# Forget logits of a hybrid attention layer taken with the sink heads' values, and their cumulative sums spread by transfers

## The reference

```python
proj = x @ w_in
fq, fk, fv = ...                      # 8 heads x 64 each, forgetting attention
ff = proj[..., OFF_FF:OFF_SQ] + b_forget      # 8 columns: one forget logit per head and token
sk = rope(...)                        # 2 key heads x 64 of the sink (sliding-window) group
sv = ...                              # 2 value heads x 64 of the same group

c = cumsum(log_sigmoid(ff), axis=tokens)
s = q.k * scale + c[query] - c[key]   # causal, then softmax, then times fv
```

## Time and profile before

| | |
|---|---|
| time, median of 3 runs | 2770.1 us (2766.78 to 2772.87) |
| time of the profiled execution | 2776.75 us |
| its span | 2774.9 us |
| TensorE busy | 2598.7 us (94%) |
| VectorE busy | 2251.6 us (81%) |
| ScalarE busy | 912.4 us (33%) |
| GpSimd busy | 1309.0 us (47%) |
| first scores of pair 0 (end of the first stage) | 95.97 us after the start |

### The profile page before, as it was taken

One profiled execution on the slowest core, in us unless ns is written; L12 is line 12 of the kernel. 1 busy time (PEld: TensorE's weight loads), 2 busy tenths in 40 slices (PEclk: granted clock), 3 DMA queues, 4 the chain that ended last, 5 costly groups with the idle time before them and its releaser, 6 DMA issues.

```text
span 2774.9 us, 45831 instructions
## 1 busy us (share of the span) xinstructions
PE 2598.7 (94%) x17059; PEld 1687.8 (61%) x17251; DVE 2251.6 (81%) x4526; ACT 912.4 (33%) x1606; POOL 1309.0 (47%) x864
## 2 busy tenths in 40 slices
PE   8999979999988877899999999999999999999996
PEld 3677646689977765555565565565564564664653
DVE  4244556658789999788989988988998999999998
ACT  3333334521125556432222232232232322331324
POOL 2110010000034442266766766766666677676772
PEclk9999989999999999999999999999999999999998
DMA  4000212320103355999999999999999999999995
GB/s 165 24 16 17 84 61 98 131 99 14 38 22 130 133 209 220 326 382 361 359 353 382 355 355 351 365 373 354 347 375 356 365 373 372 345 380 367 348 342 208
DMA packets 277917, 690.68 MB, mean 249 GB/s; under 512 B 29896, under 2 KB 112328, under 8 KB 273488
## 3 DMA queue, kind: packets, MB, share of 16 engines
q0 software_dynamic: 110592, 402.70, 38.6%
q1 hardware_dynamic: 167120, 285.25, 29.0%
HBM read 626.99 MB, written 60.88 MB: 248 GB/s over the span
## 4 chain that ended last, share of the span: by engine, by line
PE 27%; DVE 19%; DMA 15%; issue 12%; POOL 3%; ACT 1%; SPq 1%; DVEq 0%; ACTq 0%; POOLq 0%
PE h_psum L1748 9%; DMA early<-u_blocks 6%; PE o_psum L2228 6%; PE r_t_psum L1211 5%; PE g_psum L2228 4%; DVE early L2069 3%; DMA early<-v_blocks,pick_index 3%; DVE rt_hot L1647 3%; POOL early L1755 2%; DMA early<-v_blocks 2%; PE h_psum L1261 2%; DVE wide L2073 2%; DMA early<-u_rows,pick_index 2%; DMA fetched<-u_rows,pick_index 1%; DVE early L1738 1%
## 5 line engine op out<-in xcount | busy, mean ns | idle before, releaser
L1748 PE MATMUL h_psum<-early 128*128 128x384 bf16 x5496 | 767.3, 300 | 6.6 <-DVE early L1738 3.4
L1748 PEld LDWEIGHTS h_psum<-early 128*128 128x128 bf16 x5496 | 537.7, 98 | 234.3 <-issue 10.1
L1755 POOL DMA_INDIRECT early<-u_rows,pick_index x320 | 456.9, 1428 | 227.8 <-DVE dots L2069 142.3
L1755 POOL DMA_INDIRECT early<-v_blocks,pick_index x320 | 459.5, 1436 | 199.3 <-DVE wide L2073 117.3
L2228 PE MATMUL o_psum<-v_split,w_split 128*128 128x512 bf16 x2293 | 543.0, 382 | 1.6 <-issue 0.2
L2073 DVE SCALAR_TENSOR_TENSOR wide<-early,dots,wide 128x1024 f32<-128x1024 f32 x320 | 405.5, 1279 | 23.5 <-DMA early<-v_blocks,pick_index 22.0
L2069 DVE CUSTOM_DVE_ANT_0 early<-early,wide 128x1024 f32<-128x1024 f32 x320 | 386.9, 1218 | 30.3 <-DMA early<-u_rows,pick_index 27.5
L2228 PEld LDWEIGHTS o_psum<-v_split,w_split 128*128 128x128 bf16 x2304 | 227.2, 99 | 277.2 <-issue 9.1
L2228 PE MATMUL g_psum<-v_split,w_split 128*128 128x512 bf16 x1399 | 348.8, 384 | 35.6 <-DVE w_split L2035 12.6
L2228 PEld LDWEIGHTS g_psum<-v_split,w_split 128*128 128x128 bf16 x1536 | 150.0, 98 | 198.0 <-issue 31.1
L1947 ACT ACTIVATE v_split<-early 128x512 bf16<-128x512 f32 x256 | 159.0, 622 | 320.9 <-PE o_psum L2228 217.5
(11 more groups left out here) (230 smaller groups left out, 3335.1 us busy)
## 6 DMA issues: line engine op xcount, KB each, us to landing
early<-v_blocks SPq DMA_DIRECT2D x256, 256.0 KB, 6.4
early<-u_blocks SPq DMA_DIRECT2D x115, 512.0 KB, 8.4
gates<-wide SPq DMA_DIRECT2D x20, 2048.0 KB, 6.4
gate<-gates SPq DMA_DIRECT2D x31, 1280.0 KB, 21.4
early<-w_query SPq DMA_DIRECT2D x8, 1024.0 KB, 5.9
rt_u_pre<-u_blocks SPq DMA_DIRECT2D x13, 512.0 KB, 4.0
early<-w_fox SPq DMA_DIRECT2D x4, 1536.0 KB, 6.4
early<-u_rows,pick_index POOLq DMA_INDIRECT x320, 8.3
```

Source lines behind the costliest of these rows:

```text
L1748: mm = pe.matmul(bank(half)[:, 0:width * P], u_split[:, k, part, c], xs[:, first:first + width, xpart, c, :], start=(c == 0 and part == 0 ...
L1755: pool.indirect_dma_start(row, None, source, bass.IndirectOffsetOnAxis(ap=pick_index[:, tile, at:at + 1], axis=0)).then_inc(arrived, 16)
```

## The change

Host side: `b_forget` is handed over repeated for the eight token tiles, `minus_row` is gone, and there is a DRAM scratch tensor `neg_c_rows` of 8 x 1024 fp32. In the first stage:

- The first loop of TensorE makes the keys alone. The forget weights stand beside the value weights in `w_vf` (136 columns), so that the values' matmuls bring 8 logits for each tile of tokens, with tokens on partitions; three tiles share a bank.
- The value and forget weights have a semaphore of their own, `w_vf_in`; `const_in` counts eight loads.
- Softplus runs on 128 partitions x 64 columns. Eight transposes then bring it to 8 partitions x 1024 in `s_psum[1]`, from where the scan reads it. Sums now have the sign of `neg_c`, and `c_col` is copied with scale -1.
- SP stores the scan's rows to `neg_c_rows` and loads each row back with a broadcast over 128 partitions; VectorE waits for two heads ahead of pair 0 (`bias_in[0]`) and for six ahead of pair 1.
- Odd chunks of pair 0's projection go to `t_psum[1]`, even ones to `p_psum`; a chunk of pair 0 waits for the copy of the chunk two before it.
- The rotation stands ahead of chunk 0; the projection's other five chunks are one run.

```diff
+VF = P + FOX_HEADS
+VF_TILES = 3
...
+        vf_psum = [bank[:, 0:VF_TILES * VF].rearrange("p (t n) -> p t n", n=VF)
+                   for bank in (t_psum[0], t_psum[1], s_psum[0][:, 0])]
...
+        def chunk_bank(pair, chunk):
+            return t_psum[1] if pair == 0 and chunk % 2 else p_psum
...
             def _(sp):
-                sp.dma_start(w_f_raw[:, :, :], w_forget).then_inc(w_first_in, 16)
...
-                sp.dma_start(w_kv_raw[:, 1], w_skv[:, 1]).then_inc(const_in, 16)
-                sp.dma_start(b_f[:, :], b_forget).then_inc(const_in, 16)
+                sp.dma_start(w_kv_raw[:, 1], w_skv[:, 1]).then_inc(w_vf_in, 16)
+                sp.dma_start(w_f_raw[:, :, :], w_forget).then_inc(w_vf_in, 16)
+                sp.dma_start(f_bias, b_forget.partition_broadcast(P)).then_inc(const_in, 16)
...
-                sp.dma_start(minus_row, consts["minus_row"]).then_inc(const_in, 16)
...
                 for n in range(3):
                     load_weights(n)
+                sp.wait_ge(first_ready, 2)
+                sp.dma_start(neg_c_rows, c_row).then_inc(c_stored, 16)
+                sp.wait_ge(c_stored, 16)
+                for h in range(FOX_HEADS):
+                    sp.dma_start(neg_c[:, h], neg_c_rows[h].partition_broadcast(P)).then_inc(bias_in[int(h >= 2)], 16)
...
             def _(pe):
-                        if c == 0 and past(n):
-                            pe.wait_ge(chunk_copied, n)
+                        if c == 0 and n > 1:
+                            pe.wait_ge(chunk_copied, n - (n < FOX_CHUNKS))
...
-                        f_mm = products(s_psum[0][0:FOX_HEADS, half], lambda a: w_f[:, a, c], x_half,
-                                        c == 0, c == KD - 1)
-                        k_mm = products(s_psum[1][:, half], lambda a: w_kv[:, a, 0, c], x_half,
-                                        c == 0, c == KD - 1)
+                        mm = products(s_psum[1][:, half], lambda a: w_k[:, a, c],
+                                      lambda b: xt[:, b, c, half * 512:half * 512 + 512], c == 0, c == KD - 1)
...
-                        mm = products(t_psum[t // 4][:, t % 4 * P:t % 4 * P + P],
-                                      lambda a: xt[:, a, c, t * P:(t + 1) * P], lambda b: w_kv[:, b, 1, c],
+                        mm = products(vf_psum[t // VF_TILES][:, t % VF_TILES],
+                                      lambda a: xt[:, a, c, t * P:(t + 1) * P], lambda b: w_vf[:, b, c],
                                       c == 0, c == KD - 1)
...
-                project_fox(0, 0, 0, KD)
-                pe.wait_ge(const_in, 16 * 10)
...
+                project_fox(0, 0, 0, KD)
+                pe.wait_ge(f_step, 7)
                 pe.wait_ge(first_ready, 1)
-                for h in range(FOX_HEADS):
...
-                        mm = pe.matmul(s_psum[h % 2][:, half], minus_row[:, h], c_row[:, half * 512:half * 512 + 512],
-                                       start=True, stop=True)
-                    mm.then_inc(bcast_done, 1)
-                    project_fox(0, 0, 2 * KD + h * KD // 2, 2 * KD + (h + 1) * KD // 2)
+                for t in range(TILES):
+                    mm = pe.transpose(s_psum[1][0:FOX_HEADS, t // 4, t % 4 * P:t % 4 * P + P], f_rows[:, t], ident)
+                mm.then_inc(first_made, 1)
+                pe.wait_ge(first_copied, 7)
+                project_fox(0, 0, KD, FOX_CHUNKS * KD)
+                pe.wait_ge(first_ready, 2)
...
             def _(dve):
+                dve.wait_ge(first_copied, 1)
+                dve.tensor_tensor(sk_t[:, :], raw[:, :], cos[:, :], ALU.mult).then_inc(rope_step, 1)
+                dve.wait_ge(first_copied, 4)
+                dve.tensor_tensor(f_flat, f_flat, f_bias, ALU.add).then_inc(f_step, 1)
...
+                dve.wait_ge(first_made, 3)
+                dve.tensor_tensor(rope_tmp[:, :], s_flat[1], sin[:, :], ALU.mult).then_inc(rope_step, 1)
+                dve.wait_ge(rope_step, 2)
+                dve.tensor_tensor(sk_t[:, :], sk_t[:, :], rope_tmp[:, :], ALU.add).then_inc(first_ready, 1)
+                dve.wait_ge(f_step, 6)
+                dve.tensor_tensor(f_flat, f_tmp, f_flat, ALU.subtract).then_inc(f_step, 1)
+                dve.wait_ge(first_made, 4)
...
+                dve.tensor_tensor_scan(c_row, s_flat[1][0:FOX_HEADS], zeros, 0.0, ALU.add, ALU.add).then_inc(first_ready, 1)
...
+                    if u == 0 and pair < 2:
+                        dve.wait_ge(bias_in[pair], (32, 96)[pair])
                     dve.wait_ge(scores_done, n + 1)
...
             def _(act):
-                for h in range(FOX_HEADS):
-                    act.wait_ge(bcast_done, h + 1)
...
-                    act.activation(neg_c[:, h], s_flat[h % 2], ACT.Copy).then_inc(bcast_copied, 1)
...
+                for chunk in range(FOX_CHUNKS):
+                    copy_chunk(0, 0, chunk)
+                act.wait_ge(first_made, 5)
```

More of the change, by code:

```diff
@@ L271, in project_fox @@
                             pe.wait_ge(pair_lo, pair + 1)
-                        if c == 0 and past(n):
-                            pe.wait_ge(chunk_copied, n)
-                        half = chunk % 2
+                        if c == 0 and n > 1:
+                            pe.wait_ge(chunk_copied, n - (n < FOX_CHUNKS))
+                        bank, half = chunk_bank(pair, chunk), chunk % 2
                         if chunk < 4:
-                            mm = products(p_psum[:, :], lambda a: w_pair[:, kp, a, chunk // 2, c],
+                            mm = products(bank[:, :], lambda a: w_pair[:, kp, a, chunk // 2, c],
                                           lambda b: xt[:, b, c, half * 512:half * 512 + 512], c == 0, c == KD - 1)
@@ L507, in rope @@
                     dve.tensor_tensor(rope_tmp[:, 0:512], p_psum[:, :], sin[:, part], ALU.mult).then_inc(chunk_copied, 1)
[L508 to L509 removed]
+                    dve.tensor_tensor(local.q_t[pair][:, part], raw[:, part], cos[:, part], ALU.mult).then_inc(rope_step, 1)
+                    dve.wait_ge(rope_step, n + 3)
                     dve.wait_ge(chunk_copied, FOX_CHUNKS * PAIRS + SWA_CHUNKS * pair + 3 + half)
@@ L637, in _ @@
-                act.wait_ge(fa_step, 1)
-                act.activation(f_tmp[2], f_tmp[2], ACT.Ln, bias=1.0).then_inc(fa_step, 1)
-                act.wait_ge(first_made, 2)
-                act.activation(raw[:, :], s_flat[1], ACT.Copy).then_inc(raw_copied, 1)
-                act.wait_ge(first_made, 3)
-                for k in range(2):
-                    act.activation(sv_rows[:, 4 * k:4 * k + 4].rearrange("p t c -> p (t c)"), t_psum[k][:, :],
-                                   ACT.Copy).then_inc(raw_copied, 1)
@@ L645, in _ @@
[L645 to L654 removed]
+                        act.wait_ge(w_first_in, 16)
@@ new lines, in _ @@
+                        act.activation(w_k[:, 0], w_kv_raw[:, 0], ACT.Copy).then_inc(w_hi, 1)
+                act.wait_ge(w_vf_in, 32)
+                act.activation(w_vf[:, 0, :, 0:P], w_kv_raw[:, 1], ACT.Copy).then_inc(w_hi, 1)
+                act.activation(w_vf[:, 0, :, P:VF], w_f_raw[:, :, :], ACT.Copy).then_inc(w_hi, 1)
+                act.wait_ge(first_made, 1)
+                act.activation(raw[:, :], s_flat[1], ACT.Copy).then_inc(first_copied, 1)
+                act.wait_ge(first_made, 2)
@@ new lines, in _ @@
+                for k, bank in enumerate(vf_psum):
+                    tiles = slice(VF_TILES * k, min(VF_TILES * (k + 1), TILES))
+                    act.activation(f_rows[:, tiles], bank[:, 0:tiles.stop - tiles.start, P:VF], ACT.Copy
+                                   ).then_inc(first_copied, 1)
+                for k, bank in enumerate(vf_psum):
+                    tiles = slice(VF_TILES * k, min(VF_TILES * (k + 1), TILES))
+                    act.activation(sv_rows[:, tiles], bank[:, 0:tiles.stop - tiles.start, 0:P], ACT.Copy
+                                   ).then_inc(first_copied, 1)
```

126 lines of the change are left out of this document (44 added, 82 removed).

## The result

The changed kernel takes 2732.3 us (median; 2725.4 to 2737.2) against 2768.4 for the kernel before on the same occasion; the ratio is 0.9866, 95% interval 0.9844 to 0.9888.

What follows compares the result with a forecast made beforehand. TensorE's own work list was taken to bound the first stage; 0.45 + 12.05 - 0.7 + 16.4 - 1.0 + 0.2 = 27.4 us, taken as 27.3, gives 2770.1 - 27.3 = 2742.8 us. Range 2737 to 2753 us, 77 in 100.

Steps and rivals of the forecast that it cites:

- Key loop: TensorE's first loop without forget products: ends at 22.2 us instead of 34.7, bounds 22.0 to 23.6; 12.05 in the sum.
- Values with 136 columns: Value matmuls carrying the forget logits: 11.6 us instead of 10.9, a cost of 0.7 us, ending at 33.8.
- Rotation and chunk 0: Behind the values: rotation some 1.9 us, chunk 0 5.0 to 5.1 us, no wait for POOL's first split, margin 1.6.
- Spread by matmul: TensorE's per-head spreads among pair 0's chunks go: 2.05 us a head, 16.4 us for eight, the largest term.
- Second bank: Own bank for pair 0's odd chunks: prevents a new wait of about 0.7 us at each of four boundaries.
- Spread by DMA: SP's store and broadcasts, first two heads in at about 64 us, needed at 69.3: cost taken as zero.
- biases late: Rival, 7 in 100: broadcasts ahead of pair 0 as slow as under load, first bias at 73.5 us, time 2747 us.
- Port held by POOL: Rival, 7 in 100: late softplus subtraction held until POOL's second split ends at 49.4; 8.9 us given back, 2752 us.
- Clock: Rival, 3 in 100: pauses in the first loop keep TensorE at 1.2 GHz until the first scores; slower, 2799 us.
- Sum: All first-stage terms: 27.4 us by addition, 27.2 by the clock of pair 0's first bias, 27.3 taken.
- 3 us either way for a median of three runs (2766.8 to 2772.9): Allowance in the forecast range for uncertainty of the starting time, the median 2770.1 us.
- nothing in this stage is a share of the whole: Ground for taking the first-stage saving worked out in the profiled execution, unscaled, from the median of the runs, 2770.1 us.

Runs made afterwards that it cites:

- e1: The changed kernel as it is, run again against the kernel before: ratio 0.9875 (0.9836 to 0.9913).
- e9: The changed kernel as it is, another repeat against the kernel before: ratio 0.9885 (0.9853 to 0.9918).
- e4: The kernel before with its matmul spreads and their copies cut to 128 of 1024 columns, leaving wrong biases: ratio 0.9948 (0.9921 to 0.9974) to the kernel before.
- e7: The changed kernel with all chunks of pair 0 in one bank: ratio 0.9910 (0.9882 to 0.9938) to the kernel before.
- e8: The changed kernel with the eight broadcasts issued from head 7 down to head 0: ratio 0.9907 (0.9884 to 0.9931) to the kernel before.
- e5: The kernel before, making forget products for the first slice of x alone: ratio 0.9949 (0.9926 to 0.9973) to the kernel before.
- e6: The changed kernel with ScalarE waiting for all constants before casting the values' weights: ratio 0.9926 (0.9900 to 0.9951) to the kernel before.
- the first comparison: The changed kernel's first measurement against the kernel before: 2732.3 us against 2768.4, ratio 0.9866 (0.9844 to 0.9888).
- e10: The changed kernel as it is, another repeat against the kernel before: ratio 0.9886 (0.9851 to 0.9920).
- e3: The kernel before plus only the changed kernel's DRAM scratch and one awaited store to it: ratio 0.9985 (0.9960 to 1.0010) to the kernel before.
- e2: The changed kernel with 128 additional 512-column matmuls on TensorE ahead of chunk 1: ratio 1.0003 (0.9977 to 1.0030) to the kernel before.
- e11: The changed kernel with 128 additional 512-column matmuls ahead of chunk 1, a repeat: ratio 0.9984 (0.9962 to 1.0007) to the kernel before.
- e12: The changed kernel with 512 additional 512-column matmuls ahead of chunk 1: ratio 1.0304 (1.0266 to 1.0343) to the kernel before.

## Why the prediction was right in the stage and wrong in the number

- **Which stage, and what bounds it:** right. TensorE's list stayed without a gap, and first bias and end of list moved together.
- **Key loop:** forecast to end at 22.2, the values began at 21.9. 36 of its matmuls in e1 went in 7.95 us (14.19 to 22.14), 0.66 us for three, so the additional 0.1 us of the earlier trace rows did belong to the alternation with the 8-row weights. TensorE started at 8.86, 0.5 earlier than the 9.35 assumed.
- **Values with 136 columns:** 11.35 us (21.88 to 33.23), forecast 11.6. **Rotation and chunk 0:** 2.0 and 5.0 us, no wait for POOL in this trace. The margin of 1.6 us was too thin to count on: it was 1.0 here, and in e1 and e9, where the weights landed later, TensorE waited 0.42 us. **Transposes:** 0.9 us to the next chunk, forecast 1.0. **Chunks 1 to 5:** 26.35 (41.06 to 67.41), forecast 26.0.
- **Spread by matmul, 16.4:** 16.1 by chunks 1 to 5 of the two traces, and e4 measures 1.5 of the 2.05 a head by itself. **Second bank:** 0.86 a boundary in e7, forecast 0.7.
- **Spread by DMA at nothing:** right. The store was followed by the first broadcast at 55.5 (forecast 57.5). The rival "biases late" had some 6 us of room in the order chosen: in e8 all eight were in at 71.35, six heads of 512 KB at 394 GB/s are 8.0 us, and the first broadcast was issued 0.6 later than in the changed kernel, which puts the first two at 62.8 there, an estimate, against 68.8.
- **Port held by POOL:** the wait of TensorE didn't come, since the chain ended 5.5 us clear of POOL's second subtraction. But the working left out the first one: the chain's first operation was held behind it in all four traces of the changed kernel, by 0.3 to 1.6 us, and only the chain's margin of about 2 us hid that. e5 shows the full price where the chain slips.
- **Clock:** the fear of a slow stage was wrong, since all from 14.1 us on went at full pace. The recorded 1.00 doesn't fit the start of the first loop, though: 11 matmuls of 512 columns fill 4.64 us there, 0.42 each, as at the lower level, while the earlier trace rows has this slow pace only until 12.58. It cost nothing, for x was awaited. Pauses of 2 and 4 us in e5 and e6 lowered the clock for a few microseconds, not for a stage.

```profile
8.86:13.50 4.64, 4.64 (x11) 1.64 (x12) 1.91 (x2) 1.84 (x3) 0.00 (x0) 1.00 1.03 418
```

- **Sum:** first bias forecast at 69.5, measured 68.8: 27.95 us saved there for 27.3. "Should reach the end nearly whole": 26.6 arrive at the end of routing.

The step that failed is the last one, from the stage to the time, with two terms in it. The first is the starting time and its room, "3 us either way for a median of three runs (2766.8 to 2772.9)", the spread of those three. Single executions of this kernel have a standard deviation of 7.4 us, and up to the end of routing traces of the same code agree within 1.4 us, so nearly all of it arises behind the routing. The three came out 4.6 high, and starting from 2765.5 the same saving gives 2738. The range should have had some 6 us either way for that alone: 5 for a median of three and 3.7 for a result of four executions, added as squares. The 5.5 us given as what a measurement can tell from no change is likewise less than one deviation of a single execution. The second term is "nothing in this stage is a share of the whole", which takes the expert phase as equal in both kernels: the saving over 22 and 71 executions is 32.2 us and not 27.3. The 10.5 us between 2742.8 and 2732.3 are then 4.6 of the start, 4.9 of the saving, and 1.0 by which the result's four executions lie below the mean of 22. That the start was high is chance, and it alone would have left the result inside the range; the additional saving is what no part of the working had.

What is left open is the cause of these 4.9 us, whose standard error is 1.5. That is over three standard errors, and by the means of their own occasions the differences are 37.0 (the first comparison), 32.0 (e1) and 32.2 (e9 and e10), so chance is an unlikely cause. Put as the expert phase alone (mean time, less 1.8 us outside the span, less the end of routing in the trace), the kernel before has 1634.8 us (standard error 0.9) and the changed kernel 1628.9 (1.2). Between them lie the scratch alone (e3) with 1631.9 (2.4), the delayed kernels with 1632.4 (e2 and e11, 1.7) and 1633.3 (e12, 4.0), and the changed kernels with their stage made longer (e6, e7, e8) with 1633.3 (1.6). Those three average 20.9, 23.5 and 26.4 us below the 2765.5 of before, where their traces have 20.0, 22.6 and 23.2 at the end of routing. The two kernels that leave out values have 1628.4 (e4, 1.6) and 1624.4 (e5, 2.8), though they have the code of before behind the stage; so a shorter phase isn't the changed kernel's alone, unless their wrong values cause it there. Layout, instruction list and time of the start each showed no effect beyond some two standard errors, and no trace locates the 4.9 us.

## What to carry to other kernels

Before a saving of a per cent is forecast, find the part of the kernel whose length changes from one execution to the next: here the first stage repeats within 1 us, while the expert phase, with a DMA share of 0.97 from 1140 us to the end, spreads over 20, so the range belongs to the latter and the sum to the former. A small operand that rides with a large one (8 columns on 128) cost 0.4 us here (11.35 for 10.94), while as weights of its own it took a full pass of x, some 12 us. When work that covered a copy or a landing is taken away, list what it covered: a second bank was worth 3.5 us here and a semaphore of its own 5.7, of which 1.5 was a late landing.

## What the runs showed of the hardware

- Behind a 2 us wait of TensorE (e5) and a 4 us wait (e6) its granted clock was 0.54 over 7.5 us and 0.57 over 4 us, costing 3 and 1.6 us on top of the wait. In e5 TensorE had been busy for only 4.5 of the 6 us from 47 to 53, which takes in the start of its wait.
- VectorE with two SBUF operands and POOL's subtraction held each other up both ways, and the recorded duration holds the wait: POOL's second subtraction took 9.05 us in e5 instead of 6.34, where VectorE's scan of two SBUF operands had begun ahead of it. The scan itself took 4.72 us instead of 2.28 and ended 2.14 us behind POOL's cast (40.54 to 43.28).
- Reading one 4 KB row of DRAM into 128 partitions, eight times in a row, ran at 394 GB/s in the densest stretch of the changed kernel:

```profile
60.00:64.00 4.00, 4.00 (x75) 4.00 (x73) 0.00 (x0) 0.60 (x1) 0.00 (x0) 1.00 1.02 394
```
